# Rearranged passes of the mix, blocks and rotations, and a fourth slot for weights as they land

## The chip, the cores and the metric

The kernel runs on one core of one Trainium2 chip. The core has a matrix engine (PE), a vector engine (DVE), a scalar engine (ACT), a further vector-like engine (POOL) and SP, which here only issues transfers. Their instruction streams run side by side and meet at semaphores. The metric is the device time of one execution in microseconds (us), as a median over runs.

## What is computed

256 tokens of width 1024 pass through two stacks of two layers each, in float32. The first stack is a hybrid layer: many projections of one normalized input, three attentions (one windowless causal, one over the 64 best keys that an index score picks, one over a memory of 256 rows), each gated, then merged and added to x.

```python
h = rmsnorm(x, norm_g)
proj = jnp.einsum('bsd,dc->bsc', h, w_in)
...
ys = jnp.stack([ya, yb, ym], axis=2)
up = jnp.einsum('bsnw,nwd->bsnd', ys, w_branch)
gates = jax.nn.sigmoid(mix.reshape(b, s, N_BRANCH, D_MODEL))
return x + jnp.einsum('bsd,de->bse', jnp.sum(gates * up, axis=2), w_out)
```

The second stack projects x once and mixes it three ways: gated linear attention (GLA), a delta-rule recurrence (RWKV-7), and a sparse attention (NSA) whose output is a gated sum over compressed blocks, selected blocks and a window. Then comes the output projection, a layer norm, a gated feed-forward part and another layer norm. In short, with the reference's names:

```python
o_gla = (_head_norm(o, ln_w, ln_b, H, LN_EPS) * jax.nn.silu(g)).astype(dt)
o_rwkv = ((_head_norm(y, ln_w, ln_b, H, RWKV_GN_EPS) + bonus) * g).astype(dt)
o_nsa = gt[..., 0:1] * o_cmp + gt[..., 1:2] * o_slc + gt[..., 2:3] * o_win
mix = jnp.concatenate([o_gla, o_rwkv, o_nsa], axis=-1) @ w_out[l]
x = _layer_norm(DEEPNORM_ALPHA * x + mix, ln1_w[l], ln1_b[l])
ffn = (jax.nn.silu(x @ ffn_w_gate[l]) * (x @ ffn_w_up[l])) @ ffn_w_down[l]
x = _layer_norm(DEEPNORM_ALPHA * x + ffn, ln2_w[l], ln2_b[l])
```

## The kernel before

**Weights.** All weights are streamed in tiles of 128x1024 (512 KB). SP loads tile i into one of RAW slots (L157) once the tile RAW places earlier is no longer needed. ACT rounds it into a high part (L172, "cast"), POOL subtracts to get the low part (L179), and PE multiplies high by high, low by high and high by low (L210): twelve passes of 512 columns for a full tile and both token tiles. High and low parts lie in SPLIT = 4 slots, so ACT's cast of a tile waits until PE has used the tile four places back. Where a tile's cast stands in ACT's program is written out by hand: `W.high` and, around it, `pace` and `casts`.

**First stack.** The steps of the projection are computed one after the other into two PSUM banks in turn (PJ), one per token tile; ACT's `take` copies them out (L715). Step ("in", 11) is a narrow one of 364 columns. `acc` and `bbias` hold index scores and the mask of the 64 best, `ra` and `rb` the temporaries of the rotation.

**Second stack.** DVE turns the projected columns into rotated keys (`roped(4, ...)`) and queries (`roped(5, ...)`), and makes running sums of the decays (`summed`), whose exponentials ACT takes. PE transposes the queries (`in_step_6`, L1283). The "mix" is a hand-written order on all engines: attention group a goes through scores (PE), scaled scores and their maximum (DVE `soft`), exponentials (ACT `exps`, L1982), a transposition (PE `turn_p`, L1464), a copy (ACT `turned_p`) and values (PE L1480); `nsa(a)` is scores a, turning a-1, values a-2. The compressed blocks have a softmax of their own (`block_soft`, exponential at L2074, `block_sums`), a turning (`block_turn_p`), and an output per token tile that is added into NS (`block_output`). `outcome` adds the other two parts of NSA into NS. `centre`, `spread`, `deviation` and `scale` are the head norm of GLA and RWKV-7; PE transposes its result Y ("y"), ACT applies weight and bias of the norm in PSUM (`weighted`, L2114), and DVE gates it and splits it into a high and a low part (`mixed`, L2584). `turn_n` transposes NS; `n_high` and `n_low` split it. In this part slots 1 to 3 of the split weights serve as scratch memory.

## Time and profile before

| | us |
|---|---|
| median of three runs | 1549.4 (1549.4 to 1552.5) |
| the profiled execution | 1543.2 |
| its span | 1541.6 |
| PE busy | 1495.2 |
| POOL busy | 961.6 |
| ACT busy | 779.3 |
| DVE busy | 701.9 |

The profiled execution is one of its own, a little faster than the timed ones; durations are read from it. Its mean granted clock is 0.993. A row of the timeline gives the start, the duration and, in brackets, how long the engine stood before it and what released it. Matmuls overlap, so the distance between two starts tells the pace, not the duration. A line such as L1283 belongs to a helper, so many places share it.

### The profile page before, as it was taken

The numbers are of one execution on the slowest core, as the hardware profiler recorded it, in microseconds if no ns is written. First come the engines' busy times: TensorE is split into PE (matmuls) and PEld (weight loads), VectorE is DVE, ScalarE is ACT, GpSimd is POOL, SyncE is SP. The second block draws the span as 40 slices with busy tenths as digits, with TensorE's granted clock in tenths as the row PEclk, the third lists the DMA queues.
The fourth block names the chain that finished last, engine by engine and source line by source line (L and its number), as shares of the span: only waits on it lengthen the run. The fifth ranks groups of instructions, "written<-read, shape, count | busy, mean of one in ns | idle before, by whom it ended". The sixth has DMA issues, their size and how long they took to land. (4 is left out here: it accounts for less than half of the span.)

```text
span 1541.6 us, 20723 instructions
## 1 busy us (share of the span) xinstructions
PE 1495.2 (97%) x7896; PEld 1232.6 (80%) x7896; DVE 701.9 (46%) x1092; ACT 779.3 (51%) x1232; POOL 961.6 (62%) x416
## 2 busy tenths in 40 slices
PE   7999999999999999999999999999999999899997
PEld 6888788878887888788788768888788797688886
DVE  3222865472137762645665851110347667612112
ACT  5544665445445665358444444443477344454342
POOL 6887538888885468877200278878774002488785
PEclk9999999999999999999999999999999999999999
DMA  7666326555664346565311157655553311366563
GB/s 237 170 184 178 110 84 177 173 173 164 195 178 123 110 124 221 178 189 151 118 56 56 55 151 221 188 156 193 168 161 111 110 56 55 109 178 182 147 199 128
DMA packets 121633, 227.97 MB, mean 148 GB/s; under 512 B 10304, under 2 KB 26176, under 8 KB 121536
## 3 DMA queue, kind: packets, MB, share of 16 engines
q1 hardware_dynamic: 120384, 222.46, 48.3%
q10 hardware_dynamic: 1152, 4.19, 0.9%
q8 instruction: 63, 1.03, 0.3%
q14 instruction: 34, 0.28, 0.1%
HBM read 225.58 MB, written 1.05 MB: 147 GB/s over the span
## 5 line engine op out<-in xcount | busy, mean ns | idle before, releaser
L179 POOL TENSOR_TENSOR parts<-raw,parts 128x1024 fp32r<-128x1024 f32 (+5 forms) x412 | 961.4, 2346 | 565.5 <-ACT parts L172 563.3
L210 PE MATMUL ps<-parts,xT 128*128 128x512 f32 (+4 forms) x2624 | 810.2, 386 | 9.6 <-ACT H L715 3.0
L172 ACT CAST parts<-raw 128x1024 fp32r<-128x1024 f32 (+5 forms) x412 | 416.0, 1012 | 430.1 <-PE ps L210 252.7
L210 PEld LDWEIGHTS ps<-parts,xT 128*128 128x128 f32 x2624 | 487.2, 188 | 114.1 <-issue 5.2
L210 PE MATMUL ps<-parts,x_low 128*128 128x512 f32 (+3 forms) x672 | 251.2, 382 | 0.0
L210 PE MATMUL ps<-parts,M_low 128*128 128x512 f32 (+2 forms) x640 | 244.3, 386 | 0.0
L210 PEld LDWEIGHTS ps<-parts,x_low 128*128 128x128 f32 x672 | 126.7, 189 | 22.9 <-issue 0.5
L210 PEld LDWEIGHTS ps<-parts,M_low 128*128 128x128 f32 x640 | 120.4, 188 | 20.3
L210 PE MATMUL ps<-parts,aT 128*128 128x512 f32 x352 | 109.8, 395 | 0.6 <-POOL parts L179 0.6
L210 PE MATMUL ps<-parts,H_low 128*128 128x512 f32 x272 | 106.0, 394 | 0.0
L210 PEld LDWEIGHTS ps<-parts,aT 128*128 128x128 f32 x352 | 66.0, 187 | 16.7 <-POOL parts L179 1.1
L2725 DVE TENSOR_TENSOR EE<-ps,EE 128x512 f32<-128x512 f32 (+1 forms) x24 | 15.5, 647 | 102.6 <-ACT EE L2164 102.6
L210 PE MATMUL ps<-parts,ysT 128*128 128x512 f32 x192 | 61.4, 396 | 0.4 <-DVE sm L1002 0.4
L210 PEld LDWEIGHTS ps<-parts,H_low 128*128 128x128 f32 x272 | 51.1, 188 | 12.1
L2662 DVE SCALAR_TENSOR_TENSOR ps<-x,ps 128x512 f32<-128x512 f32 x16 | 11.1, 696 | 108.3 <-PE ps L210 107.0
L2732 DVE TENSOR_TENSOR H<-ps,EE 128x512 f32<-128x512 f32 (+1 forms) x24 | 15.5, 647 | 95.8 <-PE ps L210 95.8
L715 ACT ACTIVATE H<-ps,st 128x512 f32<-128x512 f32 (+2 forms) x72 | 47.1, 666 | 23.0 <-PE ps L210 23.0
L778 ACT ACTIVATE sm<-sm,nmx 128x256 f32<-128x256 f32 (+1 forms) x80 | 36.3, 455 | 25.9 <-DVE nmx L957 25.9
L210 PE MATMUL ps<-parts,mn_high 128*128 128x512 f32 x128 | 43.9, 411 | 0.4 <-DVE mn_low L832 0.4
L210 PEld LDWEIGHTS ps<-parts,ysT 128*128 128x128 f32 x192 | 36.1, 188 | 9.5 <-issue 1.2
L1283 PE MATMUL ps<-ident,H 128*128 128x128 f32 x228 | 32.6, 275 | 7.2 <-DVE H L2185 6.0
L878 DVE COPY QKT<-ps 128x512 f32<-128x512 f32 x20 | 13.8, 691 | 53.8 <-PE ps L518 53.6
(351 smaller groups left out, 1802.3 us busy)
## 6 DMA issues: line engine op xcount, KB each, us to landing
raw<-in_w_in SPq DMA_DIRECT2D x160, 512.0 KB, 3.6
raw<-in_ffn_w_down SPq DMA_DIRECT2D x44, 512.0 KB, 4.5
raw<-in_ffn_w_gate SPq DMA_DIRECT2D x40, 512.0 KB, 3.7
raw<-in_ffn_w_up SPq DMA_DIRECT2D x40, 512.0 KB, 3.7
raw<-in_w_out SPq DMA_DIRECT2D x32, 512.0 KB, 3.5
raw<-in_w_branch SPq DMA_DIRECT2D x24, 512.0 KB, 3.4
raw<-in_w_mem_kv SPq DMA_DIRECT2D x16, 512.0 KB, 3.5
raw<-in_w_in SPq DMA_DIRECT2D x16, 366.0 KB, 3.2
```

The lines of the kernel that those rows point to most:

```text
L172: self.nc.scalar.copy(self.part(i, 0)[:, 0:nk, 0:w], self.raw(i)[:, 0:nk, 0:w]).then_inc(self.hi_ready.sem, 1)
L179: self.nc.gpsimd.tensor_tensor(self.part(i, 1)[:, 0:nk, 0:w], self.raw(i)[:, 0:nk, 0:w], self.part(i, 0)[:, 0:nk, 0:w], ALU.subtract).then ...
L210: ins = pe.matmul(b[:, 0:w], a(k0 + 2 * n + c, t), self.part(i, lo_w)[:, c, 0:w], start=(opens and n == p == 0), stop=(final and p == len( ...
L715: PJ.empty(lane, nc.scalar.activation(H[:, t, c0:c0 + w], b[:, 0:w], ACT.Sigmoid if s in TAIL_STEPS else ACT.Copy, scale=st[:, 0, t:t + 1] ...
L778: lane.done(nc.scalar.activation(smv(a, j), smv(a, j), ACT.Exp, bias=nmx[:, a, j:j + 1], accum_out=den[:, a, j:j + 1]), p_ok if j == 3 els ...
L878: ins = v.tensor_copy(QKT[:, use[1], 2 * use[2]:2 * use[2] + 2, :], turned(b))
L1283: ins = pe.transpose(b[:, k * P:(k + 1) * P], src, chip.ident[:])
L2662: lane.done(v.scalar_tensor_tensor(out=b, in0=x[:, t, j * HALF:(j + 1) * HALF], scalar=ALPHA, in1=b, op0=ALU.mult, op1=ALU.add))
L2725: PJ.empty(lane, v.tensor_tensor(sg[:, t, 0:w], b[:, 0:w], sg[:, t, 0:w], ALU.mult), (("gt", j), t))
L2732: ins = v.tensor_tensor(H[:, t, c0:c0 + w], b[:, 0:w], sg[:, t, 0:w], ALU.mult)
```

## The change

It does five things. RAW goes from 3 to 4; the room comes from laying `acc`, `bbias`, `ra`, `rb`, `BP` and one of the two states `SP` over other tiles. In the first stack ACT takes token tile 0 of ("in", 11) before the cast that stood ahead of it. In the second stack the rotations of the queries go ahead of the sums of GLA's decays, and ACT's exponentials of these sums go behind the gate's sigmoid; `BP` now lies over small weights, so DVE waits for one more bank before writing it. `block_sums` moves ahead of `gla_scale(4)` and also multiplies the block probabilities by their factors, so that `block_output` is one addition instead of a product and an addition. The affine step of the head norm with the gates, g * (w * y + b), is made with a gain WG and a shift BG that ACT prepares earlier in eight passes (`gains`; one product of the shift with RWKV's gate is left to DVE), so `weighted` goes and `mixed` has two passes in place of three. Last, DVE's last sum of NSA (`nsa(13)`) goes ahead of `spread(0)`.

```diff
-RAW = 3
+RAW = 4
...
+LAST_NARROW = ("in", 11)
...
-        acc = sb("acc", [P, NT, S])
-        bbias = sb("bbias", [P, NT, S])
...
+        acc, bbias = (KV[:, n, 0:HALF].rearrange("p (t s) -> p t s", t=NT) for n in range(2))
...
+                        closes = W.begin(s) + n == W.end(s) and s[0] in ("in", "mem")
+                        ahead = closes and s == LAST_NARROW
+                        if ahead:
+                            take(s, 0)
                         W.high(act, W.begin(s) + n + SPLIT - 1)
-                        if W.begin(s) + n == W.end(s) and s[0] in ("in", "mem"):
-                            for t in range(NT):
+                        if closes:
+                            for t in range(1 if ahead else 0, NT):
                                 take(s, t)
...
                 def block_turn_p():
-                    pe.wait_ge(*E("pc_exp").at(1))
+                    pe.wait_ge(*E("mxc").at(2))
...
                 def turn_n(t):
-                    pe.wait_ge(*E("ns").at((1, 1 + len(SUMS2) // 4)[t]))
+                    if t == 0:
+                        BO.taken(pe, ("block", 0))
+                    else:
+                        pe.wait_ge(*E("ns").at(len(SUMS2) // 4))
...
+                def gains(g, c0):
+
+                    for c in range(2):
+                        w, b = (vec[:, v0 + c0 + c:v0 + c0 + c + 1] for v0 in (V_LNW, V_LNB))
+                        lane.done(sc.activation(WG[:, c0 + c, :], g[:, c, :], ACT.Copy, scale=w))
+                        if c0:
+                            lane.done(sc.activation(BG[:, c0 + c, :], BON[:, c, :], ACT.Identity, bias=b), E("shifts"))
+                        else:
+                            lane.done(sc.activation(BG[:, c, :], g[:, c, :], ACT.Copy, scale=b), E("shifts"))
...
-                nsa(7)
+                turned_p(6)
+                gains(GT, 2)
+                exps(7)
                 W.high(act, first)
-                nsa(8)
+                turned_p(7)
+                act.wait_ge(*E("gg_ok").at(1))
+                gains(FT[:, F_GG:F_GG + 2, :], 0)
+                exps(8)
...
+                TP.drained(dve, ("mg",))
                 tt(BP[:, :, :], BB[:, :, :], EN[:, :, :], ALU.mult, E("tilde"))
...
+                    tt(pc, pc, fcc[:, :, :].unsqueeze(3).to_broadcast([P, NT, 8, NB]), ALU.mult, E("mxc"))
...
-                    BO.empty(lane, v.tensor_tensor(tmp.rearrange("p (h d) -> p h d", d=HD), b.rearrange("p (h d) -> p h d", d=HD),
-                                                   fcc[:, t, :].unsqueeze(2).to_broadcast([P, 8, HD]), ALU.mult), ("block", t))
...
-                    tt(dst, dst, tmp.rearrange("p (c g d) -> p c g d", c=4, g=2), ALU.add, None if t else E("ns"))
+                    ins = v.tensor_tensor(dst, dst, b.rearrange("p (c g d) -> p c g d", c=4, g=2), ALU.add)
+                    BO.empty(lane, ins, ("block", t))
...
-                    dve.wait_ge(*E("weighted").at(t + 1))
-                    tt(b[:, 0:2], b[:, 0:2], FT[:, F_GG:F_GG + 2, n], ALU.mult)
-                    tt(b[:, 2:4], b[:, 2:4], BON[:, :, n], ALU.add, settle=False)
-                    tt(b[:, 2:4], b[:, 2:4], GT[:, :, n], ALU.mult)
+                    tt(b, b, WG[:, :, n], ALU.mult)
+                    tt(b, b, BG[:, :, n], ALU.add)
...
+                dve.wait_ge(*E("shifts").at(4))
+                tt(BG[:, 2:4, :], BG[:, 2:4, :], GT[:, :, :], ALU.mult)
                 block_output(1)
...
                 nsa(12)
+                nsa(13)
                 spread(0)
-                nsa(13)
```

On DVE, behind the rotations of the keys in layer 0 of the second stack, stands before (LD are the log decays, CUM their running sums, "H<-arena" ends a rotation of q):

```order
L2185 TENSOR_TENSOR LD<-LD,DL 128x512
L2268 SCALAR_TENSOR_TENSOR CUM<-at_reset,LD 128x256 x2
L2185 TENSOR_TENSOR EE<-CUM 128x512
L2241 SCALAR_TENSOR_TENSOR arena<-ps,fst,at_rope_873 128x512
L2241 SCALAR_TENSOR_TENSOR arena<-ps,fst,at_rope_873 128x8x32 x2
L2185 TENSOR_TENSOR H<-arena 128x512
L2241 SCALAR_TENSOR_TENSOR arena<-ps,fst,at_rope_873 128x512
L2241 SCALAR_TENSOR_TENSOR arena<-ps,fst,at_rope_873 128x8x32 x2
L2185 TENSOR_TENSOR H<-arena 128x512
```

and now (line numbers are those of the changed kernel):

```order
L2255 SCALAR_TENSOR_TENSOR arena<-ps,fst,at_rope_873 128x512
L2255 SCALAR_TENSOR_TENSOR arena<-ps,fst,at_rope_873 128x8x32 x2
L2199 TENSOR_TENSOR H<-arena 128x512
L2255 SCALAR_TENSOR_TENSOR arena<-ps,fst,at_rope_873 128x512
L2255 SCALAR_TENSOR_TENSOR arena<-ps,fst,at_rope_873 128x8x32 x2
L2199 TENSOR_TENSOR H<-arena 128x512
L2199 TENSOR_TENSOR LD<-LD,DL 128x512
L2282 SCALAR_TENSOR_TENSOR CUM<-at_reset,LD 128x256 x2
L2199 TENSOR_TENSOR EE<-CUM 128x512
```

The three rows of the sums went behind the six of the rotations.

On ACT in the mix of the same layer, from the copy of the turned blocks (spare_2) on, stands before ("H,den<-H,nmx" are exponentials of a group, "parts<-raw" a cast):

```order
L2079 COPY spare_2_7054<-ps 128x256
L1989 COPY H<-ps 128x512
L1982 ACTIVATE H,den<-H,nmx 128x256 x2
L172 CAST parts<-raw 128x1024
L1989 COPY H<-ps 128x512
L1982 ACTIVATE H,den<-H,nmx 128x256 x2
L172 CAST parts<-raw 128x1024
```

and now (LD is the gain, EP the shift, vec2s their weights and biases):

```order
L1997 COPY H<-ps 128x512
L2107 ACTIVATE LD<-GT,vec2s 128x256
L2109 ACTIVATE EP<-BON,vec2s 128x256
L2107 ACTIVATE LD<-GT,vec2s 128x256
L2109 ACTIVATE EP<-BON,vec2s 128x256
L1990 ACTIVATE H,den<-H,nmx 128x256 x2
L172 CAST parts<-raw 128x1024
L1997 COPY H<-ps 128x512
L2107 ACTIVATE LD<-FT,vec2s 128x256
L2111 ACTIVATE EP<-FT,vec2s 128x256
L2107 ACTIVATE LD<-FT,vec2s 128x256
L2111 ACTIVATE EP<-FT,vec2s 128x256
```

Four passes came between the copy and the exponentials of each of two groups.

On DVE in the same part, behind the softmax of the blocks, from the scores of group 6 on ("H<-ps,cbias" with "nmx<-H" is a group's softmax, "H<-ps,EE" a step of the recurrence), stands before:

```order
L2196 SCALAR_TENSOR_TENSOR H<-ps,cbias 128x512
L2354 TENSOR_REDUCE nmx<-H 128x2
L2185 TENSOR_TENSOR arena<-arena,FT 128x16x16 x2
L2185 TENSOR_TENSOR arena<-CUM 128x8x32 x2
L2603 TENSOR_TENSOR H<-ps,EE 64x256
L2473 COPY_PREDICATED arena<-at_masks,ps 128x32x8 x2
L2185 TENSOR_TENSOR FT<-FT,DL 128x512
L2423 TENSOR_REDUCE denc<-spare_2_7054 128x16
L2425 RECIPROCAL facc<-denc 128x16
L2185 TENSOR_TENSOR facc<-facc,gate 128x8 x2
L2190 TENSOR_SCALAR facc<-facc,at_rowv 128x8 x2
L2196 SCALAR_TENSOR_TENSOR H<-ps,cbias 128x512
```

and now:

```order
L2210 SCALAR_TENSOR_TENSOR H<-ps,cbias 128x512
L2369 TENSOR_REDUCE nmx<-H 128x2
L2438 TENSOR_REDUCE denc<-spare_2_7053 128x16
L2440 RECIPROCAL facc<-denc 128x16
L2199 TENSOR_TENSOR facc<-facc,gate 128x8 x2
L2204 TENSOR_SCALAR facc<-facc,at_rowv 128x8 x2
L2199 TENSOR_TENSOR spare_2_7053<-spare_2_7053,facc 128x256
L2199 TENSOR_TENSOR arena<-arena,FT 128x16x16 x2
L2199 TENSOR_TENSOR arena<-CUM 128x8x32 x2
L2616 TENSOR_TENSOR H<-ps,EE 64x256
L2488 COPY_PREDICATED arena<-at_masks,ps 128x32x8 x2
L2199 TENSOR_TENSOR FT<-FT,DL 128x512
```

The four rows of the block sums went up by five rows, with a fifth row, the product with the probabilities, behind them.

## Rows read from the trace of the kernel before

**Rows 1.** The page, section 1: busy time, share of the span, instructions.
```profile
PE 1495.2 (97%) x7896; PEld 1232.6 (80%) x7896; DVE 701.9 (46%) x1092; ACT 779.3 (51%) x1232; POOL 961.6 (62%) x416
```
**Rows 2.** Waits of PE over the span: us in total, times, longest us.
```profile
PE ps L1283 <- DVE H L2185: 6.0, 4, 2.2
...
PE ps L210 <- ACT H L715: 3.0, 3, 1.4
PE ps L1464 <- ACT H L1982: 2.6, 4, 0.7
PE ps L210 <- DVE x_low L2584: 1.8, 2, 0.9
...
PE ps L210 <- POOL parts L179: 1.5, 3, 0.6
```
**Rows 3.** Timeline, narrow step: start us, us, engine, line, operation, count [idle <- releaser].
```profile
73.37 1.05 ACT L172 CAST parts<-raw 128x1024 fp32r<-128x1024 f32 x1 [1.39 <-DMA raw<-in_w_in]
74.32 1.01 ACT L715 ACTIVATE H<-ps,st 128x364 f32<-128x364 f32 x2
75.02 0.47 PE L210 MATMUL ps<-parts,xT 128*128 128x512 f32 x1 [1.38 <-ACT H L715]
75.33 0.39 PE L210 MATMUL ps<-parts,M_low 128*128 128x512 f32 x1
75.56 0.40 PE L210 MATMUL ps<-parts,xT 128*128 128x512 f32 x1
```
**Rows 4.** Timeline of DVE and PE, last projection steps of layer 0, second block.
```profile
737.23 0.69 DVE L2185 TENSOR_TENSOR LD<-LD,DL 128x512 f32<-128x512 f32 x1
737.96 2.90 DVE L2268 TENSOR_TENSOR_SCAN CUM<-at_reset,LD 128x256 f32<-128x256 f32 x2
...
741.69 1.53 DVE L2241 SCALAR_TENSOR_TENSOR arena<-ps,fst,at_rope 128x512 f32<-128x512 f32 x3
...
746.86 0.65 PE L1283 MATMUL ps<-ident,H 128*128 128x128 f32 x4 [2.18 <-DVE H L2185]
```
**Rows 5.** Timeline of DVE in the mix, around the block sums.
```profile
844.30 0.76 DVE L2185 TENSOR_TENSOR arena<-CUM 128x256 f32<-128x256 f32 x2 [4.00 <-PE ps L1333]
...
847.16 0.41 DVE L2423 TENSOR_REDUCE denc<-spare 128x16 f32<-128x256 f32 x1
...
848.18 0.36 DVE L2190 TENSOR_SCALAR facc<-facc,at_rowv 128x8 f32<-128x8 f32 x2
```
**Rows 6.** Timeline: ACT's nearest row to a gain pass; block output, exponentials and turnings.
```profile
708.97 0.74 ACT L1927 ACTIVATE FT<-FT 128x256 f32<-128x256 f32 x2
...
853.49 1.65 DVE L2185 TENSOR_TENSOR H<-H,IC 128x512 f32<-128x512 f32 x1
...
856.72 0.51 ACT L1982 ACTIVATE H<-H,nmx 128x256 f32<-128x256 f32 x1 [3.42 <-DVE nmx L2354]
...
857.87 0.66 PE L1464 MATMUL ps<-ident,H 128*128 128x128 f32 x4 [0.59 <-ACT H L1982]
...
877.05 0.66 PE L1283 MATMUL ps<-ident,H 128*128 128x128 f32 x4 [1.00 <-DVE H L2185]
```
**Rows 7.** Timeline of ACT and PE at the end of the mix.
```profile
888.92 1.48 ACT L2114 ACTIVATE ps<-ps,vec2s 128x128 f32<-128x128 f32 x4 [0.83 <-PE ps L1283]
...
893.22 0.50 PE L210 MATMUL ps<-parts,xT 128*128 128x512 f32 x1 [0.88 <-DVE x_low L2584]
```
**Rows 8.** Timeline of POOL and DVE while both work.
```profile
858.82 4.76 POOL L179 TENSOR_TENSOR parts<-raw,parts 128x1024 fp32r<-128x1024 f32 x2 [4.24 <-ACT parts L172]
...
859.68 1.52 DVE L2185 TENSOR_TENSOR fac<-fac,gate 128x4 f32<-128x4 f32 x1
```
**Rows 9.** ACT's waits in the down projection (1035 to 1090); POOL's full tiles, grouped.
```profile
ACT parts L172 <- DMA raw<-in_ffn_w_down: 33.9, 20, 2.5
...
L179 POOL TENSOR_TENSOR parts<-raw,parts 128x1024 fp32r<-128x1024 f32 x356 | 864.0, 2440 | 519.7 <-ACT parts L172 517.9
```
**Rows 10.** Windows, 836 to 842: busy us of PE, PEld, DVE, ACT, POOL; granted clock, DMA.
```profile
836.00:842.00 6.00, 6.00 (x24) 5.17 (x25) 2.98 (x6) 1.88 (x6) 0.00 (x0) 0.52 0.01 3
```

More of the change, by code:

```diff
@@ L425, in first_layers @@
         mn_lo = sb.over("mn_low", "PT", [P, KC, S])
-        acc = sb("acc", [P, NT, S])
-        bbias = sb("bbias", [P, NT, S])
-        ra, rb = acc[:, :, :].rearrange("p t s -> p (t s)"), bbias[:, :, :].rearrange("p t s -> p (t s)")
+        acc, bbias = (KV[:, n, 0:HALF].rearrange("p (t s) -> p t s", t=NT) for n in range(2))
+        ra, rb = (sm[:, 1, 2 * n:2 * n + 2, :].rearrange("p a s -> p (a s)") for n in range(2))
         ikd = sb("ikd", [P, NT, P])
@@ L1123, in second_layers @@
         BB = sb("BB", [P, 2, S])
-        BP = sb("BP", [P, 2, S])
+        BP = sw[:, 0:2, :]
         DL = sb("DL", [P, 10, S])
@@ L1959, in _ @@
                 casts(("in", 5), 3)
-                act.wait_ge(*E("cum_g").at(1))
-                lane.done(sc.activation(EP[:, 0:2, :], CUM[:, 0:2, :], ACT.Exp, scale=1.0 / 16), E("exps"))
-                lane.done(sc.activation(EE[:, 0:2, :], EE[:, 0:2, :], ACT.Exp, scale=1.0 / 16), E("exps"))
                 casts(("in", 6), 0)
@@ L1974, in _ @@
                 lane.done(sc.activation(gate[:, :, :], H[:, :, NGT:NGT + 24], ACT.Sigmoid), E("gate"))
+                act.wait_ge(*E("cum_g").at(1))
+                lane.done(sc.activation(EP[:, 0:2, :], CUM[:, 0:2, :], ACT.Exp, scale=1.0 / 16), E("exps"))
+                lane.done(sc.activation(EE[:, 0:2, :], EE[:, 0:2, :], ACT.Exp, scale=1.0 / 16), E("exps"))
                 def exps(a):
@@ L2110, in _ @@
                 n_high(1)
-                def weighted(t):
-                    b = TP.read(act, ("y", t))
-                    for c in range(4):
-                        ins = sc.activation(b[:, c * P:(c + 1) * P], b[:, c * P:(c + 1) * P], ACT.Identity,
-                                            scale=vec[:, V_LNW + c:V_LNW + c + 1], bias=vec[:, V_LNB + c:V_LNB + c + 1])
-                        lane.done(ins, E("weighted") if c == 3 else None)
-                weighted(0)
                 squares(1)
@@ L2312, in _ @@
                     roped(4, t, K_AT, 384, NKC, E("k_roped"))
+                for t in range(NT):
+                    roped(5, t, 0, 512, NQ, E("q_roped"))
                 dve.wait_ge(*E("lnz").at(1))
@@ L2315, in _ @@
                 summed(0)
-                for t in range(NT):
-                    roped(5, t, 0, 512, NQ, E("q_roped"))
                 def blocks(kv, use):
@@ L2628, in _ @@
                 soft(6)
+                block_sums()
                 gla_scale(4)
```

9 lines of the change are left out of this document (4 added, 5 removed).

## The prediction

> **What bounds the kernel now.** The page's first section says it: the matrix engine (PE) is busy for 97% of the span, DVE, ACT and POOL far less [rows 1]. So a change pays only where PE stands, and only as much as it stands there. I read next the list of waits for PE alone [rows 2]. Five lines of it are what this change can reach: PE waits for ACT's copy out of a projection bank (L715, 3.0 us in 3 waits), for DVE's sums before a turning (L2185, 6.0 us in 4 waits), for the exponentials (L1982, 2.6 us in 4), for the lower parts of the mixed output (L2584, 1.8 us in 2), and for POOL's split of a weight tile (L179, 1.5 us in 3). That is 14.9 us, and no edit that leaves the matmuls alone can win much more: PE's instructions are the same in number and order. The other waits of PE (start, layer norms) hang on chains that the diff does not touch. Then I read the timeline around each of these waits, in the first of the two layers, since the second repeats it nearly to a tenth.
>
> **Step 1, the narrow projection step.** PE starts its last narrow pass near 73.3, and ACT could read tile 0 then, but it first casts a weight tile (73.37, after 1.39 us of waiting for the transfer) and only then takes both banks (74.32, 1.01 us for two); PE stands 1.38 us at 75.02 [rows 3]. The change takes tile 0 ahead of that cast. Tile 0 is finished six narrow passes before tile 1, so its copy (half of 1.01 us) ends before PE wants the bank. Tile 1's copy comes behind the cast: 1.05 + 0.5 us after it, while PE has six full passes of 0.23 us on tile 0 (starts 75.33 and 75.56), 1.4 us, plus the six narrow ones. Queued behind the new wait on ACT are that cast and the POOL split behind it, which PE reaches two weight tiles later. Three waits, 3.0 us in all; the third is the wider step before it, and there only the earlier transfer of step 4 helps. I take 2.7 us, bounds 1.5 and 3.0.
>
> **Step 2, rotations ahead of the sums.** DVE does one subtraction (0.69 at 737.23), two scans (2.90) and one more subtraction of the same size, then from 741.69 the rotations of q, 1.53 for three operations and some 0.7 for the addition, twice; PE stands 2.18 us at 746.86 for the second [rows 4]. With the four operations of 4.3 us behind the rotations, q is ready about 4.3 us earlier, so the wait goes with 2 us to spare. One limit is that tile 1 of this step must be out of PE first; that costs at most the second rotation's own 2.3 us after it. Next late would be the weights of the same step, which are cast earlier here too, as ACT no longer waits for the sums between two casts. What is pushed back are the sums and ACT's two exponentials of them, which now come behind the gate's sigmoid; their reader, DVE's decayed keys, comes some 20 us later. The added wait for the bank of the gates stands before one multiplication of 0.69 us, and DVE then waits for ACT's next copy anyhow. The four waits for these sums come to 6.0 us [rows 2]: this one in each layer, 4.4, and the one at 877.05 in each layer, the other 1.6. Of the 4.4 I take 4.3 us, bounds 2.5 and 4.4.
>
> **Step 3, the mix.** (a) The block sums (L2423 to L2190, from 847.16 to 848.54, 1.4 us) and one new multiplication of about 0.42 us move from after the scores' softmax into a hole in which DVE waits 4.00 us for PE [rows 5]. About 1.9 us of work fits, even behind the exponential that ACT makes at the start of that hole. PE's turning of the blocks now waits for the sums, and comes in PE's order after the scores whose end closes the hole at 844.30; the sums are ready by 843. So the move costs nothing, and frees 1.3 us of DVE ahead of the next softmax. If the hole were gone the turning would wait up to 1.9 us in each layer. (b) The block outputs lose a pass and write with one operand in PSUM; before, the second one took 1.65 us although it handles 512 elements, as 0.69 us elsewhere [rows 6]. (c) ACT gets eight passes of 128x256 ahead of two sets of exponentials. The nearest row is 0.74 us for two [rows 6], so 1.5 us for four. Both fours stand where ACT waits for DVE's maxima, the second time 3.42 us: hidden, ending a little before the maxima are there, since DVE is earlier by (a) and (b). (d) With that, of the waits for exponentials (0.59 at 857.87 [rows 6], the longest 0.7 [rows 2]) I take 2.0 of 2.6 us, bounds 0 and 2.6. (e) The last sum goes ahead of the variance, so the wait at 877.05 (1.00 us here [rows 6]) loses about 0.9 us of variance work (a reduction of 512 and two short ones) and the rest by the earlier start: 1.5 us of the two layers' 1.6, bounds 0.8 and 1.6. What it costs: the variance is later by about 1.3 us, and with it ACT's root and the copy n_high queued behind it, for which PE's third pass group waits: 0.3 us a layer, 0.6 us lost, bounds 0 and 1.2. (f) At the end ACT's four passes (1.48 us) are gone from between the turning of y and DVE, and DVE's three passes over 256 elements become two over 512, about 0.1 us more; PE stood 0.88 us at 893.22 for just this [rows 7]. Net 1.4 us earlier, more than the wait: 1.8 us of 1.8, bounds 1.2 and 1.8.
>
> A sentence of its own on contention. DVE's multiplication of four elements took 1.52 us and ended at 861.20, the moment at which the first of POOL's two subtractions (4.76 us from 858.82) ended [rows 8]. The Trainium skill, GPSIMD Engine Reference, section Specifications, gives the rule: POOL's SBUF interfaces are shared with VectorE, with contention for DVE instructions that have two SBUF inputs. By that rule the new product of the shift and the gate (both in SBUF, 128x512) can wait up to one subtraction in each layer, and the block output, which now reads PSUM, no longer can. That matters for (d) alone: 2.0 us if the product falls between two subtractions, about 0.6 if not; that it removes one collision and adds another is why I do not take the full 2.6.
>
> **Step 4, the fourth slot.** In the down projection ACT waits 33.9 us in 20 waits for transfers, yet PE stands for POOL three times in the whole kernel, 0.6 us at the longest [rows 2, 9]. A slot more lets each transfer start one POOL subtraction (2.44 us) earlier. So nearly all of what it removes are ACT's waits behind which PE has split weights ready, worth nothing. I take those 0.6 us and as much again for the casts that stand before ACT's copies of x at the layer norms: 1.2 us, bounds 0 and 2.5. The initial x transfer is queued behind one weight tile more and is not wanted until well after it.
>
> **Sum.** 2.7 + 4.3 + 2.0 + 1.5 + 1.8 + 1.2 - 0.6 = 12.9 us. A wait also costs a slow restart: the starts 75.02 and 75.33 are 0.31 apart, the next 0.23 [rows 3], 0.08 us each, and some eight such waits go: 0.6 us. Together 13.5 us. Against the profiled execution, 1543.2 us (span 1541.6 and 1.6 around it), that is 1529.7; the median of the timed runs is 6.2 us above that execution, and I carry the difference over: 1549.4 - 13.5 = 1535.9 us.
>
> **The rivals.**
> The mix gives nothing: ACT's passes and the shared port keep the exponentials late, so that PE meets the same waits. Its 2.0 + 1.5 + 1.8 - 0.6 go: 1540.6 us. For it: these are waits for ACT, and ACT gets 3 us more per layer in front. Against: ACT idles longer than that where they come. 15%.
> A saved wait turns up as a later one: steps 1 and 2 are won but PE then outruns the next thing, in the recurrence of the mix where the granted clock was 0.52 between 836 and 842 [rows 10], behind small waits. A second dip there or a longer one costs some 3 us a layer: 1542 us. 12%.
> More is won: the full 14.9 us, no loss, 2.5 us of supply and the clock dip avoided: about 1530 us. 10%.
> The fourth slot does what it says but the rest is nearly cancelled, or the waits are re-formed everywhere: within 3 us of before, 1548 us. 6%.
> Slower: more writes in flight slow POOL's subtraction. POOL takes 2.44 us a tile [rows 9] and PE twelve passes of 0.23, 2.76 us. So POOL becomes the bound from 2.76 us on, and each 0.1 us beyond costs 0.1 us on each of some 356 full tiles. At 2.85 us that is 0.09 x 356 = 32 us against 13.5 won: 1568 us. Only the down projection, with its many waits for transfers, shows how near supply is; but no row shows POOL slowed that far. 3%.
>
> **How the numbers follow.** My forecast has 54%, the five rivals 15, 12, 10, 6 and 3. The range goes from 1530.0 (the best case) to 1542.5, and leaves out the last two and the outer part of the second: about 80%. A measurement of this kernel can tell about 0.2%, 3.1 us, from no change. Faster by more than that is everything but the last two and a little: 0.91; within it 0.06; slower 0.03.
>
> **What would show it.** Narrow step: a take on ACT before the cast, and the L715 waits of PE down from 3.0 us to under 0.5. Rotations: the wait for DVE before the turning of q gone, DVE's two scans after it and shorter, since POOL idles there. Mix: the block sums inside DVE's hole with no PE wait before the turning of the blocks; no PE wait on exponentials over 0.3 us; turning of n without a wait, and a somewhat longer one for n_high; no wait on L2584. Supply: ACT's waits for transfers down to a fraction of 33.9 us in the down projection while PE's time there changes by under 1 us. It would be wrong if PE's waits move to places that now show none, if the dip of the clock widens, or if POOL's mean rises past 2.7 us.

## The result: 21 us faster, more than the range allowed

| | median us | runs | lowest to highest |
|---|---|---|---|
| before | 1549.4 | 4 | 1548.3 to 1552.5 |
| after | 1528.0 | 4 | 1524.7 to 1530.3 |
| ratio | 0.9857 | | 95% interval 0.9834 to 0.9880 |

Forecast were 1535.9 us and a range of 1530.0 to 1542.5. The direction was right, the gain of 21.4 us was far above the 13.5 of the sum, and the time lies below the range. The profiled executions tell another story: 1543.2 us before, 1528.0 after (spans 1541.6 and 1526.7). That is 15.2 us, close to the sum. A second profiled execution of after, made later, took 1524.6 us, 18.6 less than before's, so a part of this nearness is chance. Still, most of what is missing lies between before's one profiled execution and its timed runs.

The page of after answers [rows 1]:

```profile
PE 1494.0 (98%) x7896; PEld 1234.6 (81%) x7896; DVE 689.1 (45%) x1088; ACT 777.3 (51%) x1230; POOL 959.1 (63%) x416
```

And the waits of PE over the whole span of after, to be read against [rows 2] (total us, times, longest):

```profile
PE ps L518 <- DMA M<-in_mem: 6.9, 2, 4.9
PE ps L1288 <- DVE x L2703: 3.2, 2, 1.6
PE ps L1455 <- DVE spare L2210: 1.5, 2, 0.9
...
PE ps L210 <- ACT KV L720: 0.9, 1, 0.9
PE ps L210 <- POOL parts L179: 0.8, 2, 0.4
PE ps L210 <- DVE x_low L2603: 0.8, 2, 0.4
```

Of the five lines of [rows 2] four are gone: no wait for the copy L715, none for DVE before the turnings of q and n (L1283 then, L1288 now), none for the exponentials, none for the lower parts of y. POOL's line fell from 1.5 us to 0.8. New are 0.8 us for the lower part of n (L2603), the loss that step 3 had named. No median in this document leaves out an execution unless the text says so.

At the narrow step ACT now does this (start us, us, engine, line; cf. [rows 3]):

```profile
72.95 0.56 ACT L715 ACTIVATE H<-ps,st 128x364 f32<-128x364 f32 x1 [1.94 <-PE ps L210]
73.41 1.04 ACT L172 CAST parts<-raw 128x1024 fp32r<-128x1024 f32 x1
74.35 0.57 ACT L715 ACTIVATE H<-ps,st 128x364 f32<-128x364 f32 x1
```

The copy of tile 0 stands ahead of the cast, and the cast no longer waits for its transfer (1.39 us in [rows 3]). PE goes on without a gap. On DVE the two scans of the decays stand behind the rotations and take 1.27 us where they took 2.90 [rows 4]:

```profile
737.31 0.78 DVE L2199 TENSOR_TENSOR H<-arena 128x512 f32<-128x512 f32 x1
738.19 0.69 DVE L2199 TENSOR_TENSOR LD<-LD,DL 128x512 f32<-128x512 f32 x1
738.92 1.27 DVE L2282 TENSOR_TENSOR_SCAN CUM<-at_reset,LD 128x256 f32<-128x256 f32 x2
```

In the mix, the block output of token tile 0, whose second pass alone took 1.65 us in [rows 6], is now one pass of 0.69. Timeline of DVE:

```profile
845.80 0.69 DVE L2452 TENSOR_TENSOR H<-H,ps 128x512 f32<-128x512 f32 x1
```

ACT's gain passes take 0.40 to 0.41 us from start to start; the last of four and the exponentials behind it, on ACT:

```profile
843.56 0.50 ACT L2109 ACTIVATE EP<-BON,vec2s 128x256 f32<-128x256 f32 x1
843.96 0.50 ACT L1990 ACTIVATE H<-H,nmx 128x256 f32<-128x256 f32 x1
```

On PE the turning behind these exponentials comes without a wait. The second row is the new wait, behind the moved variance:

```profile
846.36 0.66 PE L1469 MATMUL ps<-ident,H 128*128 128x128 f32 x4
...
871.50 0.50 PE L210 MATMUL ps<-parts,xT 128*128 128x512 f32 x1 [0.39 <-DVE x_low L2603]
```

In the down projection ACT had waited 33.9 us for transfers [rows 9]. PE does the same work some 9 us earlier now; in that window (1025 to 1080) ACT waits for PE, and once for a transfer:

```profile
ACT parts L172 <- PE ps L210: 31.2, 18, 1.7
ACT parts L172 <- DMA raw<-in_ffn_w_down: 1.4, 1, 1.4
```

PE gained nothing from this there, as was forecast: by the count of its matmuls after is ahead by 9.2 us at 1035 and by 9.2 us at 1085 of before's trace. One sign of being wrong did come: the dip of the clock, 6.8 us long in before (834.9 to 841.8), is 10.2 us long in this trace (827.1 to 837.3). In the second trace of after it is 6.8 us again.

### The profile page after: what moved, and what is told of

Its sections match the earlier page's. It is cut to its first block and busy times, and to the rows that moved or that the text cites. A ratio compares the mean times of both kernels' runs of the same rounds, so it can differ in the third digit from the quotient of the medians.

```text
span 1526.7 us, 20723 instructions
## 1 busy us (share of the span) xinstructions
PE 1494.0 (98%) x7896; PEld 1234.6 (81%) x7896; DVE 689.1 (45%) x1088; ACT 777.3 (51%) x1230; POOL 959.1 (63%) x416
## 5 line engine op out<-in xcount | busy, mean ns | idle before, releaser
L715 ACT ACTIVATE H<-ps,st 128x512 f32<-128x512 f32 (+2 forms) x72 | 47.5, 668 | 31.7 <-PE ps L210 31.7
L1288 PE MATMUL ps<-ident,H 128*128 128x128 f32 x228 | 32.6, 275 | 1.3 <-issue 1.1
```

The costliest lines, as they stand in the source:

```text
L715: PJ.empty(lane, nc.scalar.activation(H[:, t, c0:c0 + w], b[:, 0:w], ACT.Sigmoid if s in TAIL_STEPS else ACT.Copy, scale=st[:, 0, t:t + 1] ...
L1288: ins = pe.transpose(b[:, k * P:(k + 1) * P], src, chip.ident[:])
```

## The question, and the theories

Where do some 8 us come from that the sum does not have? Three theories. **Clock and chance:** before's timed runs hold stalls and stretches of half clock which its one profiled execution does not show, and which the change removes. **A mis-sized term:** one part gives more than its term, the fourth slot first of all. **The layout:** the tiles laid over others help by themselves.

In every comparison before was run again. PE's 7,896 matmuls come in the same order in most of these kernels, so the start of the same matmul in two traces tells where one falls behind the other. "After" below is the changed kernel; its eight executions in two comparisons have a median of 1526.6 us (1524.4 to 1530.3), and where a variant is weighed against that and not against an after of its own comparison, about 2 us are uncertain.

## Experiment 1: before once more

No edit.

> The kernel before once more, unchanged. Open is the 6.2 us by which its timed runs (1549.4) lie above its profiled execution (1543.2). Theory A: it belongs to this kernel. Its stalls of PE let the granted clock dip more often or longer in most executions than in the profiled one; the runs here come to 1548 to 1550 again, each with a mean granted clock of 0.989 to 0.990 (after's own four executions went by about 1.4 us per 0.001 of clock), and a second profiled execution near 1549 would show a dip more than the first. Rival B: the earlier timed runs were high by chance or by the chip; here the median is 1543 to 1545 at a clock near 0.993, and the changed kernel's gain shrinks to about 15 us, close to the sum of 13.5.

Measured: 1548.3 us, before in the same comparison 1548.8 (17 runs, 1543.2 to 1552.4). The profiled execution of 1543.2 stands at the lower edge: of the 84 timed executions of before in the four comparisons, three are as low. (An 85th, in this run, took 2475.9 us at a mean granted clock of 0.554; nothing on record explains it, and the median moves by 0.4 us or less with it.) The mean granted clock of the 17 runs goes from 0.988 to 0.992 with a median of 0.990; the three above 1550 us have 0.988, 0.988 and 0.991. After's first four runs have 0.990 (the slowest, 1530.3) to 0.994 (the fastest, 1524.7). Rival B falls and theory A stands, but not whole: of the difference between the two traces a good part is stalls, not clock. The new trace (execution of 1549.8, span 1548.4, 6.8 us longer than the one that I had) shows what an execution near the median has. Its waits of PE:

```profile
PE ps L1283 <- DVE H L2185: 6.0, 4, 2.2
PE ps L1283 <- DVE x L2688: 3.2, 2, 1.6
PE ps L210 <- ACT H L715: 3.0, 3, 1.4
PE ps L210 <- DVE EE L2725: 2.6, 2, 1.3
PE ps L1464 <- ACT H L1982: 2.6, 4, 0.7
```

The fourth line is in no row of the trace behind the prediction. Here is how it comes about, in the feed-forward part of layer 0 (start us, us, engine, line; in brackets idle time before it and what ended that):

```profile
941.16 1.05 ACT L172 CAST parts<-raw 128x1024 fp32r<-128x1024 f32 x1 [1.63 <-DMA raw<-in_ffn_w_up]
...
942.11 1.08 ACT L2164 ACTIVATE EE<-ps 128x512 f32<-128x512 f32 x2
...
942.80 1.29 DVE L2725 TENSOR_TENSOR EE<-ps,EE 128x512 f32<-128x512 f32 x2 [11.67 <-ACT EE L2164]
...
943.64 0.47 PE L210 MATMUL ps<-parts,xT 128*128 128x512 f32 x1 [1.29 <-DVE EE L2725]
```

ACT waits 1.63 us for a transfer, casts, and only then comes to the sigmoids (L2164); DVE's product with them frees the bank for which PE stands. In the first profiled execution the same cast came in time, the sigmoid followed at 937.93, and PE had no gap:

```profile
936.97 1.05 ACT L172 CAST parts<-raw 128x1024 fp32r<-128x1024 f32 x1 [1.16 <-DMA raw<-in_ffn_w_up]
...
937.93 0.59 ACT L2164 ACTIVATE EE<-ps 128x512 f32<-128x512 f32 x1
...
939.55 0.48 PE L210 MATMUL ps<-parts,xT 128*128 128x512 f32 x1
```

The second difference is the clock. Both executions stand 2.17 us before the turning of q in the last layer. Windows of 2 us behind it (busy us of PE, PEld, DVE, ACT, POOL, granted clock, DMA share, GB/s), first the new execution:

```profile
1186.00:1188.00 2.00, 0.63 (x5) 0.63 (x6) 1.79 (x4) 0.11 (x1) 0.76 (x1) 1.00 0.15 23
1188.00:1190.00 2.00, 2.00 (x9) 1.95 (x8) 1.42 (x3) 0.59 (x1) 0.00 (x0) 0.57 0.66 240
1190.00:1192.00 2.00, 2.00 (x10) 1.84 (x8) 0.00 (x0) 0.00 (x0) 0.00 (x0) 0.57 0.00 0
```

and the first one:

```profile
1183.00:1185.00 2.00, 1.36 (x9) 1.37 (x10) 1.86 (x3) 0.59 (x1) 0.03 (x1) 1.00 0.48 117
1185.00:1187.00 2.00, 2.00 (x14) 1.79 (x13) 0.72 (x2) 0.02 (x1) 0.00 (x0) 1.00 0.36 145
```

The same kernel and the same stall: once the clock falls to 1.2 GHz for 3.4 us behind it (1188.3 to 1191.7), which costs 1.6 us, and once it does not. In microseconds by which the start of the same matmul is later than in the first trace of before:

| up to (us of the first trace) | before again | slot alone (exp. 5) | after |
|---|---|---|---|
| start (35) | +0.3 | -0.3 | +0.8 |
| first narrow step (90) | +0.2 | -2.4 | -1.4 |
| second layer's (420) | +0.2 | -4.5 | -3.5 |
| projection, second stack (735) | -0.7 | -4.5 | -4.8 |
| turning of q (750) | -0.7 | -4.8 | -7.1 |
| half of the mix, with its dip (845) | +0.7 | -3.4 | -5.7 |
| mix (900) | +0.7 | -3.7 | -8.8 |
| layer norm (912) | +2.6 | -4.0 | -9.1 |
| gate steps (950) | +4.1 | -4.0 | -9.2 |
| next projection (1110) | +3.8 | -4.9 | -10.1 |
| its last step (1182) | +3.7 | -5.0 | -12.4 |
| behind it (1200) | +5.3 | -4.9 | -12.4 |
| mix (1340) | +5.2 | -3.9 | -15.1 |
| end | +6.9 | -5.4 | -14.9 |

So the ordinary execution has 1.4 us for a longer dip at 840, 1.8 us at the layer norm (PE's wait for xT is 0.59 instead of 0.34 us, and a dip follows at 905), twice 1.5 us for EE, and 1.6 us for the dip at 1190.

## Experiment 2: three slots again

```diff
-RAW = 4
+RAW = 3
```

> The changed kernel with three slots for weights in place of four, all other edits kept. The prediction's step 4: the fourth slot is worth 1.2 us (0 to 2.5), so 1529.2 us (1528 to 1530.5) against the changed kernel's 1528.0, with ACT's waits for transfers back at over 100 us but PE's wait for POOL's parts up by under 2 us. Rival: the gain that the sum lacks (21.4 measured, 13.5 summed) is supply, the fourth slot is worth 5 us or more, so 1533 us or more, with new waits of PE for POOL in the down projection. Second rival: more writes in flight cost something, and three slots are faster, 1526.

Measured: 1531.3 us (1530.9 to 1535.6), 4.7 above after. That is outside the 1.2 us (0 to 2.5) of step 4; by size the rival was nearer, by mechanism it was not. Its trace has an EE wait of 1.4 us and waits for xT of 1.2 us (0.5 in after), but its wait for POOL is the 0.8 us of after: the slot does not work through weights that reach PE late.

## Experiment 3: rotations behind the sums again

```diff
+                act.wait_ge(*E("cum_g").at(1))
+                lane.done(sc.activation(EP[:, 0:2, :], CUM[:, 0:2, :], ACT.Exp, scale=1.0 / 16), E("exps"))
...
-                for t in range(NT):
-                    roped(5, t, 0, 512, NQ, E("q_roped"))
                 dve.wait_ge(*E("lnz").at(1))
                 tt(LD[:, 0:2, :], LD[:, 0:2, :], GQt[:, :, :], ALU.subtract)
                 summed(0)
+                for t in range(NT):
+                    roped(5, t, 0, 512, NQ, E("q_roped"))
```

> The changed kernel with the rotations of the queries behind the sums of the decays again, and ACT's exponentials of them in their old place. The prediction's step 2: PE stands some 2.2 us for the turning of the queries again in each layer, 4.3 us in all and 0.2 for two restarts, so 1532.5 us (1530.5 to 1533). Theory A (a stall also brings a dip of the granted clock in many executions): a dip stands near the wait in 1 or 2 layers, its clock is 0.001 to 0.003 lower than the changed kernel's 0.992, and the time is 1534 to 1536. Rival: the move is worth less, since tile 1 leaves PE late: 1530 or less.

Measured: 1531.5 us (1531.2 to 1536.0), 4.9 above after. The wait is back:

```profile
PE ps L1288 <- DVE H L2199: 4.0, 2, 2.2
```

Here too the clock dips behind one of the two stalls (1173.7 to 1177.1) and not behind the other. Step 2 with its 4.3 us is confirmed, and part of the rest is clock.

## Experiment 4: the narrow copy behind the cast again, with four slots and with three

```diff
-LAST_NARROW = ("in", 11)
+LAST_NARROW = None
```

> The changed kernel with ACT's copy of the narrow step's tile 0 behind the cast again. The prediction's step 1: 1.4 us in each of two layers, 2.7 us in all, less what the fourth slot keeps (the 1.39 us for which ACT waited for the transfer ahead of that cast are gone with it), so 1529 to 1530.7 us. Rival C: the fourth slot alone removes the whole stall, since the cast no longer waits; then 1528.0, no change, and the wait of PE for ACT's copy does not return. Theory A (a stall also costs clock): 1531 to 1533 with a dip near 75 us.

> The changed kernel with three slots and ACT's copy of the narrow step behind the cast, so both of the edits that can remove the stall at the narrow step are undone. Theory F: either of the two alone removes it, so undoing the copy alone cost nothing (1526.4 us) and undoing both costs the slot's 3.3 and the stall's 2.7: 1534 us (1533 to 1535.5), with 3.0 us of waits of PE for the copy (L715). Rival: the copy's stall is worth less than its length since PE catches up later; then 1531 to 1532, as with three slots alone (1531.3).

Measured: with four slots 1526.4 us (1523.9 to 1527.9), with three 1537.0 (1534.4 to 1539.8). With four slots the copy's place is worth nothing that can be measured (rival C), with three 5.7 us (1537.0 against 1531.3, from two comparisons), more than the 1534 expected. Of these the two traces show 2.8 in the first stack; in the rest there are EE waits (2 instead of 1) and a lower clock (0.990 to 0.993 for one, 0.991 to 0.994 for the other), which were not priced one by one. ACT with four slots and the copy behind the cast:

```profile
71.44 1.06 ACT L172 CAST parts<-raw 128x1024 fp32r<-128x1024 f32 x1 [0.94 <-PE ps L210]
72.44 0.56 ACT L715 ACTIVATE H<-ps,st 128x364 f32<-128x364 f32 x1
```

The cast waits for nothing but PE's slot of split weights, and is over before tile 0 is there. Two edits remove the same stall; either will do.

## Experiment 5: the fourth slot alone

All other edits are undone; the layout that makes its room stays.

> The kernel before with the fourth slot for weights (and the tiles laid over others that make its room), and no other edit. Theory D: with three slots a cast that waits for its transfer keeps ACT from the sigmoids and copies queued behind it, in most executions at the feed-forward part's fifth group and at the layer norm, in the profiled one not. The slot is then worth the 3.3 us that taking it out of the changed kernel cost, and the narrow steps' 3.0 us as well, since there too the cast waited for a transfer: 1541 to 1543 us from before's 1548.8, and PE's waits for ACT's copy (L715) are gone although the copy still stands behind the cast. The prediction's own step 4: 1.2 us, so 1547.6, with the L715 waits there. Rival: 10 us or more, 1538 or less, supply is nearly all of what the sum lacked.

Measured: 1536.9 us (1535.9 to 1537.6), 12.4 below before, at clocks of 0.992 to 0.993. That is the rival's number; theory D's 1541 to 1543 was missed by 4 us. It is half of the whole gain or a little more (24.3 us in the same comparison, 21.4 in the first) and ten times the 1.2 us of step 4. Its waits of PE still have those of the sums and the mix, and no line for L715 or EE:

```profile
PE ps L1288 <- DVE H L2200: 5.3, 4, 2.2
...
PE ps L1469 <- ACT H L1987: 2.8, 4, 0.7
PE ps L210 <- DVE x_low L2600: 1.8, 2, 0.9
```

## Experiment 6: the mix back

Gains, block sums and outputs and the last sum as before (the edits of the change's diff in reverse), the rest of the change kept.

> The changed kernel with all three edits of the mix undone (the gated norm's weights and gates, the block sums and outputs, the last sum behind the variance), with the fourth slot, the narrow copy and the rotations kept. The prediction's step 3: 2.0 + 1.5 + 1.8 - 0.6 and some restarts, so 5.0 us: 1533.0 (1531 to 1535), with PE's waits for exponentials at 2.6 us and for the lower parts at 1.8 us again. Theory E: the waits of the mix also bring longer dips of the clock between 830 and 845 and at 1270, and 2 to 5 us more are lost, 1535 to 1538, at a granted clock of 0.990 or less. Rival: the mix edits are worth what the sum lacks as plain waits, and PE shows new waits of 8 us or more.

> The changed kernel once more, beside the three below on the same chip. Its four executions so far spread from 1524.7 to 1530.3. Theory A': its time follows the granted clock as before's does, about 1.1 to 1.4 us per 0.001, and its median is 1527 to 1529. It also tells whether the narrow step's copy is worth anything: without it the kernel took 1526.4 (1523.9 to 1527.9), so if after comes to 1526 to 1527 here the two are the same, and if it stays at 1528 or above the copy costs 1 us or more.

Measured: 1531.0 us (1530.5 to 1532.3), and after beside it 1525.0 (1524.4 to 1527.6), 2 us below what was expected of it. The mix is worth 6.0 us in that comparison, 4.4 against after's eight runs. PE's waits in the variant:

```profile
PE ps L1469 <- ACT H L1987: 2.7, 4, 0.7
PE ps L210 <- DVE x_low L2600: 1.8, 2, 0.9
...
PE ps L1288 <- DVE H L2200: 1.3, 2, 0.7
```

5.8 us, less the 0.8 that after has instead, is 5.0; step 3 had 4.7. Theory E falls: the variant's clock is no lower (0.992 to 0.994).

## Experiment 7: the slot or the order behind it?

If ACT's other work behind late casts is what costs, moving that work ahead of the casts must help without a slot. In before, with three slots:

```diff
+                        ahead = closes and s == ("in", 11)
+                        if ahead:
+                            take(s, 0)
                         W.high(act, W.begin(s) + n + SPLIT - 1)
...
                     if k == 0:
+                        x1_high(0)
                         W.high(act, first_gate + 3)
-                    if k == 0:
-                        x1_high(0)
...
-                            pace(("gt", j), lambda: sigmoids(j, [1] if j == 0 else range(NT)))
+                            pace(("gt", j), lambda: sigmoids(j, [1] if j == 0 else range(NT)), ahead=j >= 1)
```

(`ahead` makes `pace` call the sigmoids in front of its last cast.)

> The kernel before with three slots, but with ACT's work moved ahead of the cast that stood in front of it at three places: the narrow step's copy of tile 0, the sigmoids and copies at the end of the gate steps 1 to 5 of the feed-forward part, and the copy of x behind the first layer norm. Nothing of supply is changed: the casts themselves still wait for their transfers. Theory D (the fourth slot's 12.4 us alone are mostly ACT's other work that stood behind late casts, and the clock dips that these stalls of PE brought): most of it comes back here without a slot, 1539 to 1543 from before's 1549, with PE's waits for the copy (L715), for the sigmoid's product (EE) and the longer one for xT gone or small. Rival G: the slot works through supply itself, PE's wait for split weights or ACT's later casts; then only the narrow step's 3.0 us are won, 1546, or less where the casts pushed back make POOL late.

Measured: 1543.8 us (1540.2 to 1547.6), before 1549.2; ratio 0.9964 (0.9951 to 0.9978). That lies between theory D's 1539 to 1543 and rival G's 1546. Its trace has no EE wait, 0.5 us for L715 and 0.5 for xT. So 5.4 us can be had by the order alone, at the places named; that is shown. That they are a part of the slot's 12.4 is read from the traces, in which the same waits are gone with the slot. The profiled executions of this kernel and of the slot alone differ by 4.5 us: 1.9 us of it have come together by 1110, in pieces of up to 1.2 us; then 1.6 for a dip at 1180 to 1185, 1.5 for one at the last layer norm (1335 to 1345), 0.9 in the last 100 us, less 1.4 by which the other's dip in the second mix is longer. Why four slots also bring fewer dips stays open: the slot alone has the same 2.2 us stall at 1182 and no dip, the kernel of experiment 3 has four slots, that stall and a dip.

## Experiment 8: the layout without the slot

The kernel of experiment 5 with `RAW = 3`.

> The kernel before with the tiles laid over others as in the changed one (index scores, mask, rotation temporaries, one state, the decayed keys with their extra wait for a bank), but still three slots for weights. It tells the slot from the layout: the kernel with both took 1536.9, 12.4 us less than before. Theory D: the layout is worth nothing (within 1.5 us of before's 1549) and all 12.4 us are the slot's. Rival J: the layout itself helps, other banks or the shift of a wait, and this comes to 1545 or less. Rival K: the overlaid tiles cost something, 1551 or more, and the slot is worth more than 12.4.

Measured: 1548.2 us (1546.1 to 1550.6), before 1548.5; ratio 0.9998 (0.9983 to 1.0014). The layout is worth nothing, within some 2 us; the 12.4 us are the slot's. Its trace is another one near the median with three slots, with EE waits of 2.0 us, and L715 of 3.2:

```profile
PE ps L210 <- ACT H L715: 3.2, 3, 1.5
...
PE ps L210 <- DVE EE L2741: 2.0, 2, 1.5
```

## Experiment 9: the scores of group 6 behind the turning

After still has a stall of 0.6 to 0.9 us a layer before the scores of group 6 (L1455), amid a stretch at 1.2 GHz. The scores were put behind the turning and the values that follow them in PE's order:

```diff
                 def nsa(a):
-                    if a < G2:
+                    if a < G2 and a != BLOCK_AT:
                         scores(a)
...
                         values(a - 2)
+                    if a == BLOCK_AT:
+                        scores(a)
```

> The changed kernel with one move on PE: the scores of group 6, which wait 0.9 us a layer for DVE to read the block scores, go behind the turning and the values of groups 5 and 4, 1.7 us of work. Theory A (a stall of PE in the recurrence's part brings the dip that holds 1.2 GHz for some 7 us in each layer): the dip gets shorter or goes, which gives up to 3.4 us a layer beside the 0.9, so 1518 to 1523 from 1526 to 1528, at a clock of 0.995 or more. Rival H: the dip comes from what PE does before it, the many small matmuls and the wait at 825, and stays; then 1524 to 1527. Rival I: the softmax of group 6 is later by 0.8 us and the stall comes back at its turning; then no gain at all.

> The changed kernel with the move on PE of the kernel beside it, and the sigmoids and the copy of x of the feed-forward part ahead of their casts as in the first kernel of this call. With four slots the casts no longer wait for transfers, so by theory D the second part gives nothing or up to 1 us (the copy of x behind the layer norm, waits of 0.2 us, and a dip at the layer norm that shows in some executions, 1.5 us): within 1 us of the kernel beside it, perhaps less spread. Rival: the casts pushed back make PE wait for POOL, 1 to 3 us slower.

Measured: 1548.0 us (1529.0 to 1566.8, clock 0.991 down to 0.966), some 20 us lost, which none of the expectations had. Four of the twelve executions lie between 1529.0 and 1536.5, six between 1545.0 and 1552.0, two above 1566; without the three slowest the median is 1545.0. With ACT's work ahead in the feed-forward part as well it was 1548.8 (1531.2 to 1566.7), two of twelve near 1531. The stall that was filled is gone, and another has come, for ACT's copy of the turned blocks:

```profile
PE ps L1469 <- ACT spare L2089: 3.1, 2, 2.0
```

Behind it the clock falls, and stays down. Windows of 3 us, same columns as above:

```profile
835.00:838.00 3.00, 1.31 (x6) 0.68 (x5) 2.57 (x7) 1.40 (x3) 0.00 (x0) 1.00 0.00 0
838.00:841.00 3.00, 2.67 (x16) 2.59 (x17) 2.66 (x6) 2.19 (x6) 0.00 (x0) 0.70 0.00 0
841.00:844.00 3.00, 3.00 (x15) 2.46 (x15) 1.82 (x5) 2.09 (x6) 0.83 (x1) 0.50 0.00 0
...
877.00:880.00 3.00, 3.00 (x16) 3.00 (x17) 1.83 (x4) 0.00 (x0) 0.00 (x0) 0.50 0.00 0
880.00:883.00 3.00, 3.00 (x14) 2.90 (x13) 0.00 (x0) 2.13 (x3) 0.00 (x0) 0.50 0.02 5
883.00:886.00 3.00, 3.00 (x17) 2.57 (x17) 0.54 (x3) 0.24 (x1) 0.00 (x0) 0.91 0.00 0
```

For 44 us (839.2 to 883.6) PE shows no idle time at 1.2 GHz, and full speed returns 1.4 us after the 512-column passes of the weights come back at 882.18. Until then PE had the matmuls of the attention and the recurrences, nearly all of 64 to 256 columns. By the count of matmuls this execution falls 19 us behind the second trace of after between 826 and 880.

Why the new stall: in the second trace of after PE works at half clock from 828.0 to 834.8, and behind that the chain block sums (DVE), turning (PE), copy (ACT) is hidden; its copy ends at 839.57 there and at 838.18 here. Here PE is at full clock and ready at 836.3, so the chain is what is late. That the dip had been covering a wait is my reading of the two traces; no run has after's order without the dip.

## Experiment 10: both stalls filled, and ACT's part alone

PE now also takes the scores of group 7 and the values of group 5 ahead of the turnings, and ACT copies the turned blocks ahead of `decayed(5)`:

```diff
-                decayed(5)
                 between(3)
                 act.wait_ge(*E("bpt_full").at(1))
                 lane.done(sc.copy(spare[2][:, 256:512], ptb[:, 0:S]), E("bpt"))
+                decayed(5)
```

> The changed kernel with PE's stalls in this part of the mix filled at both ends: the scores of group 6 behind the turning and values of groups 5 and 4 as in the first filled kernel (1548.0 us), and now the scores of group 7 ahead of the blocks' turning and the values of group 5 ahead of the turning of group 6; on ACT the copy of the turned blocks goes ahead of the decay factor of chunk 5, which waits for DVE. Theory L (the first filled kernel lost by its new 2.0 us stall at the turning of group 6, behind which the granted clock stayed at half through 43 us of small matmuls, and for no other reason): the stall is gone, the long dip with it, and the time is 1517 to 1524 with a clock of 0.994 or more, a kernel faster than both. Rival M: the dip comes with the dense run of small matmuls itself, stall or none; then 1530 to 1550 with a wide spread as before. Rival N: the stalls move on to the next groups, 1524 to 1528.

> The changed kernel with only ACT's move of the kernel beside it: the copy of the turned blocks ahead of the decay factor. PE's order is untouched. It removes one wait of 0.24 us a layer at the turning of group 6. Theory L: about 0.5 us faster or nothing, 1525 to 1528, and the dips at 825 to 840 stay as they are, as they begin ahead of this place. Rival: the shorter wait changes how long the dip lasts, and the time moves by over 2 us either way.

Measured: 1527.7 us (1525.7, 1525.9, 1529.5 and one of 1549.6 at 0.976); ACT's part alone 1525.7 (1524.1 to 1527.3). Neither can be told from after's 1526.6, and theory L's 1517 to 1524 did not come. The trace of the first has neither of the two stalls (1.8 us less of waits), and still dips from 827.7 to 834.5. So the stall at L1455 does not set the dip: theory L is half right. The 2.0 us stall is gone, and the long dip with it in three of four executions; the fourth, 1549.6 us, looks like the long dip without the stall, but it was not traced, so rival M is not excluded. The gain of the filled waits does not appear, and the trace shows where it went: a further dip at 892.6 to 896.0, and one of 10.2 us from 1257.8 where the second trace of after has 6.8 us; at half speed these are 3.4 us. What starts the short dip is not settled; the only wait left ahead of it is one of 0.54 us at 825.01. No version was found that beats after by more than can be measured.

## Why the prediction was wrong, point by point

**What bounds the kernel.** Right: PE, and its stalls. But only its waits were summed; what the clock costs was left to a rival of 10%.

**Step 1, 2.7 us.** The size is right (3.0 us of waits gone), the reason half right. [rows 3] showed the cast waiting 1.39 us for its transfer. With the fourth slot that goes, and then the copy's place is worth nothing (experiment 4).

**Step 2, 4.3 us.** Right: 2.3 us a layer between 735 and 750 and between 1110 and 1182 of the table above, 4.9 us when undone. The scans fell from 2.90 to 1.27 us. The forecast was that they get shorter as POOL idles: POOL's last split there ends at 737.53, ahead of them, where before it ran from 737.58 to 739.72, beside the first. That first scan alone took 2.31 us before and takes 0.69 now; the second took 0.66 and takes 0.67.

**Step 3, 4.7 us.** Right: 5.0 us of waits, 4.4 to 6.0 when undone. The exponentials gave all 2.6 rather than 2.0, and n's lower part cost 0.8 rather than 0.6. The new product of shift and gate, for which step 3 held something back, met no split of POOL's: 0.69 us in either layer (854.18 and 1284.73). The second layer did not repeat the first to a tenth, as was taken: PE's wait before the turning of n was 1.00 us in one and 0.66 in the other; the term had used the right total of 1.6. DVE's product of four elements still takes 1.51 us (at 861.66) as in [rows 8], and again ends with a split of POOL's (863.15), so the contention is there, but it no longer lies on PE's path.

**Step 4, 1.2 us, bounds 0 and 2.5.** This is the step that failed: the slot measured 12.4 us alone, 4.7 on top of the narrow copy, 10.6 where the copy is behind its cast. I reasoned that ACT's waits for transfers are "worth nothing" where PE has split weights ready. That is true of the weights: PE's waits for POOL were 1.5 us and became 0.8, and in the down projection PE gained nothing. But the same ACT has sigmoids and copies queued behind the waiting cast, and PE needs those. I had named this for the copies of x (0.6 us) and not looked for the others. The one trace had no sigmoid late, but it had the narrow step, where just this happens, and 33.9 us of waits in 20 pieces in one projection said that the transfers come late by little, so that small shifts can decide. Of the 12.4 us, 5.4 can be had by moving ACT's queued work ahead of the casts; through what the other 7 come, beyond fewer dips, stays open.

**The sum and what it was put onto.** Also failed: "I carry the difference over". The 6.2 us between the profiled execution and the timed ones are not a constant. They are stalls and dips of before, most of which are gone with the slot; after's profiled execution (1528.0) is at the median of its runs. With the base of 1543.2 the forecast is 1529.7 and off by 1.7 us.

**The rivals.** "More is won" was the nearest with 1530 us, and had the avoided dip in it; it had 10% and should have had the most. "A saved wait turns up as a later one" did not happen here, but experiment 9 shows that one reordered group of matmuls was enough for it, at some 20 us rather than 6. POOL did not get slower: its full tiles took 2439 ns in the mean, against 2440.

**An account.** From before (1549) to the slot alone 12.4; of that 5.4 can be had by order and some 7 belong to the slot, part of them clock. From there to after 10 to 12: rotations 4.9, mix 4.4 to 6.0, the narrow copy 0. The median clock went from 0.990 to between 0.992 and 0.993; as a share of 1540 us that alone is, by my estimate, some 4 us.

## What to carry to other kernels

An engine's wait is free only if nothing that stands behind it in its queue is wanted soon: with each late transfer, ask what else is queued on the engine that waits, not only who reads the transferred tile. One profiled execution is one draw; where it is faster than the timed runs, the difference can hold stalls that you have not seen, and a change may remove just those, so take a second profile before summing. And where two edits cure the same stall, count it once, with the cheaper one (here the slot, which cures others too).

## What the runs showed of the hardware that I had not expected

The granted clock falls behind a stall of 2.17 us in one execution and not in another of the same kernel, and such a dip of 3.4 us outside the mix costs 1.5 to 1.8 us. Within the mix the low stretch lasted from 6.8 us (828.0 to 834.8 in the second trace of after) to 44 us (839.2 to 883.6 in experiment 9), the long one with PE busy without a gap in all of it. The Trainium skill, TensorE: Matmul & The Clock Gate, section Part 1, says that the gate goes by how busy the engine has been of late; this trace does not bear that out as far as the profile's busy time shows it, since 3.00 of 3.00 us busy stood at 0.50 for fourteen windows in a row. A half-clocked PE may hide a chain of other engines, so that filling a stall there uncovers the next one; experiment 9 suggests this and does not prove it.
